# A transformer's last block in steps of two head pairs instead of one, with another order of work on VectorE

## What is computed

```python
h = _rmsnorm(x, norm_g[l]) * (1.0 + scale[:, None, :]) + shift[:, None, :]
p = jnp.einsum('bsd,de->bse', h, w_in[l])
c_val, c_gate, c_og, ts, r_og, g_conv, g_rwkv = jnp.split(p, SPLITS, axis=-1)
# conv branch: 31 taps over time, layer norm, silu, gate, @ w_conv_out
# rwkv branch: r, k, v, decay and rate from ts; per head of 64
def step(state, inp):
    r_t, w_t, k_t, v_t, kk_t, b_t = inp
    sk = jnp.einsum('bhvk,bhk->bhv', state, kk_t)
    state = (state * w_t[:, :, None, :] - sk[..., None] * b_t[:, :, None, :]
             + v_t[..., None] * k_t[:, :, None, :])
    return state, jnp.einsum('bhvk,bhk->bhv', state, r_t)
# group norm per head, bonus, gate, @ w_rwkv_out
m = jax.nn.sigmoid(g_conv) * y_conv + jax.nn.sigmoid(g_rwkv) * y_rwkv
x = x + gate[:, None, :] * jnp.einsum('bsd,de->bse', m, w_out[l])
```

## Time and profile before

| | us |
|---|---|
| median of 3 runs | 1036.68 (1036.30 to 1037.82) |
| the profiled execution, its own time | 1036.78 |
| its span, first to last instruction | 1035.0 |
| PE busy (matmul) | 1002.3 (97%) |
| weight loads | 932.6 (90%) |
| DVE busy | 869.7 (84%) |
| ACT busy | 604.3 (58%) |
| loads from HBM | 164.83 MB |

### The profile page before, as it was taken

One profiled execution on the slowest core, in us unless ns is written; L12 is line 12 of the kernel. 1 busy time (PEld: TensorE's weight loads), 2 busy tenths in 40 slices (PEclk: granted clock), 3 DMA queues, 4 the chain that ended last, 5 costly groups with the idle time before them and its releaser, 6 DMA issues.

```text
span 1035.0 us, 25000 instructions
## 1 busy us (share of the span) xinstructions
PE 1002.3 (97%) x10690; PEld 932.6 (90%) x10690; DVE 869.7 (84%) x1447; ACT 604.3 (58%) x875; POOL 18.4 (2%) x38
## 2 busy tenths in 40 slices
PE   7999999999999999999999999999999999899997
PEld 6999999999999989989898998889999998789996
DVE  7866699899988886999899897989999999965474
ACT  7755664444446756554444577556657676686443
POOL 2000000000000000000000000000000000000000
PEclk9999999999999999999999999999999999999999
DMA  9662457777554515576775646334323422234531
GB/s 283 214 203 94 152 189 252 230 243 227 199 176 149 164 47 181 200 231 227 241 234 182 203 133 194 109 99 124 122 86 123 125 84 84 84 124 155 170 126 41
DMA packets 136075, 168.26 MB, mean 163 GB/s; under 512 B 3216, under 2 KB 125328, under 8 KB 135728
## 3 DMA queue, kind: packets, MB, share of 16 engines
q1 hardware_dynamic: 132080, 153.44, 46.1%
q0 software_dynamic: 3904, 13.50, 4.0%
HBM read 164.83 MB, written 2.10 MB: 161 GB/s over the span
## 4 chain that ended last, share of the span: by engine, by line
PE 68%; DVE 22%; ACT 6%; issue 2%; DMA 2%; SPq 0%; DVEq 0%; ACTq 0%
PE banks L353 13%; PE banks L318 8%; PE banks L319 7%; PE banks L320 7%; PE banks L355 7%; DVE hf L2652 4%; DVE w_parts L304 3%; DVE w_parts L280 3%; PE banks L655 2%; PE bank L657 2%; PE bank L655 2%; PE banks L657 2%; PE bank L659 2%; PE banks L659 2%; ACT w_parts L275 1%
## 5 line engine op out<-in xcount | busy, mean ns | idle before, releaser
L280 DVE TENSOR_TENSOR w_parts<-raw,w_parts 128x2048 fp32r<-128x2048 f32 x95 | 217.1, 2288 | 27.3 <-ACT w_parts L275 26.8
L353 PE MATMUL banks<-x_parts,w_parts 128*128 128x512 f32 x640 | 227.1, 399 | 0.0
L318 PE MATMUL banks<-x_parts,w_parts 128*128 128x256 f32 x704 | 211.9, 301 | 0.0
L319 PE MATMUL banks<-x_parts,w_parts 128*128 128x256 f32 x736 | 208.3, 283 | 0.0
L320 PE MATMUL banks<-x_parts,w_parts 128*128 128x256 f32 x704 | 199.1, 283 | 0.0
L275 ACT ACTIVATE w_parts<-raw 128x2048 fp32r<-128x2048 f32 x95 | 180.9, 1905 | 3.6 <-PE banks L810 2.1
L355 PE MATMUL banks<-x_parts,w_parts 128*128 128x256 f32 x640 | 179.8, 281 | 0.0
L353 PEld LDWEIGHTS banks<-x_parts,w_parts 128*128 128x128 f32 x640 | 120.3, 188 | 29.0
L319 PEld LDWEIGHTS banks<-x_parts,w_parts 128*128 128x128 f32 x736 | 141.2, 192 | 0.5 <-issue 0.5
L318 PEld LDWEIGHTS banks<-x_parts,w_parts 128*128 128x128 f32 x704 | 134.5, 191 | 7.6 <-issue 0.7
L320 PEld LDWEIGHTS banks<-x_parts,w_parts 128*128 128x128 f32 x704 | 134.8, 192 | 0.0
(11 more groups left out here) (418 smaller groups left out, 2411.6 us busy)
## 6 DMA issues: line engine op xcount, KB each, us to landing
raw<-in_ffn_w_up SPq DMA_DIRECT2D x44, 1024.0 KB, 5.1
raw<-in_w_in SPq DMA_DIRECT2D x36, 1024.0 KB, 5.5
raw<-in_ffn_w_down SPq DMA_DIRECT2D x22, 1024.0 KB, 5.9
big<-in_ada_w_t POOLq DMA_DIRECT2D x24, 512.0 KB, 4.1
raw<-in_gla_w_in SPq DMA_DIRECT2D x11, 1024.0 KB, 5.6
raw<-in_attn_w_qkv SPq DMA_DIRECT2D x6, 1024.0 KB, 4.9
raw<-in_gla_w_out SPq DMA_DIRECT2D x4, 1024.0 KB, 5.5
raw<-in_attn_w_out SPq DMA_DIRECT2D x4, 1024.0 KB, 4.9
```

Of the source, the lines that this page charges most:

```text
L280: eng.tensor_tensor(WL[:, n % RING, :, :], RAW[:, n % RING, :, :], WH[:, n % RING, :, :].bitcast(F32), ALU.subtract).then_inc(w_lo_ready, 1)
L318: nc.tensor.matmul(ps, wh, xh, start=start, stop=False)
L319: nc.tensor.matmul(ps, wh, xl, start=False, stop=False)
L353: nc.tensor.matmul(PS[bank + m].rearrange("p (a t) -> p a t", a=2), WH[:, s, k, ms], XP[:, :, k, :], start=k == 0, stop=False, skip_group_ ...
```

## The change

The last block goes in steps s = −2 to 4 of 13 slots, and in each step the chain, the middle and the front serve two pairs (a "duo"). Fronts of the second pair of a duo follow the first in the same step, in slots 6 to 11. Inverse masks, copies and evacuations of both pairs are made by one instruction. The blocks are dealt anew: 4, 5, 6, 6, 5 and 9 in steps −2 to 3. The hi halves stand at unit 7 of the block two earlier and unit 0 of the block before, the lo halves at units 2 and 4 of the block before. The lo of most blocks is written over the raw weights (`RAW_LO`), which frees 24 tiles (`DUO`) for the second pair; the load of block n + 3 then waits for the matmuls of block n. DVE has the front ahead of `slot(s, r)`. Taps start in slot 8 of step −2 and end with step 2. rout 0 and 1 are whole blocks behind the steps.

```diff
 STEP_BLOCKS = {
     -3: _blocks("r0 k0 v0"),
-    -2: _blocks("val0 gate0"),
-    -1: _blocks("r1 k1 v1 val1"),
-    0: _blocks("gate1 val2 rog0 gate2"),
-    1: _blocks("r2 k2 v2 val3"),
-    2: _blocks("gate3 rog1 gr0 gr1"),
-    3: _blocks("r3 k3 v3 gr2"),
-    4: _blocks("rog2 gr3 gc0"),
-    5: _blocks("gc1 gc2"),
-    6: _blocks("rog3 og0 og1 og2 og3"),
-    7: _blocks("gc3 cout0 cout1 cout2 cout3"),
-    8: _blocks("rout0 rout1 rout2 rout3 out0 out1 out2 out3"),
+    -2: _blocks("val0 gate0 k1 r1"),
+    -1: _blocks("v1 val1 gate1 k2 r2"),
+    0: _blocks("v2 val2 gate2 k3 r3 gc0"),
+    1: _blocks("rog0 v3 val3 gate3 gr0 gc1"),
+    2: _blocks("rog1 gr1 gr2 gr3 gc2"),
+    3: _blocks("rog2 gc3 og0 og1 og2 og3 rog3 cout0 cout1"),
+    4: _blocks("cout2 cout3 rout0 rout1 rout2 rout3 out0 out1 out2 out3"),
 }
...
+DUOS, SLOTS = 4, 13
+LO_IN_RAW = range(N_L3 + 3, N_ROUT + 1)
...
+        def w_lo(n):
+            return (RAW_LO if n in LO_IN_RAW else WL)[:, n % RING, :, :]
...
         def load(sp, n, src, i=0):
-            if n >= RING:
+            if n - RING in LO_IN_RAW:
+                sp.wait_ge(block_done, n - RING + 1)
+            elif n >= RING:
                 sp.wait_ge(w_lo_ready, n - RING + 1 + RING * i)
...
-        def put_blocks(s, names, last=24):
+        def put_blocks(s, names, last=2 * SLOTS):
             per = 8 * len(names)
             for b, name in enumerate(names):
                 n = PLACE[name]
                 for u in range(8):
                     q = (8 * b + u) * last // per
                     put_at(s, q, ("unit", n, u))
-                    if u % 2 == 0:
-                        put_at(s, q, ("hi" if u < 4 else "lo", n + 2, u // 2 % 2))
+                    if u == 0 and n > N_L3 + 3:
+                        put_at(s, q, ("hi", n + 1, 1))
+                    if u in (2, 4) and n > N_L3 + 3:
+                        put_at(s, q, ("lo", n + 1, u // 2 - 1))
+                    if u == 7:
+                        put_at(s, q, ("hi", n + 2, 0))
                 put_at(s, q, ("take", n))
-                put_at(s, min(q + 1, 23), ("use", n))
-
-        for s in range(-2, 8):
+                put_at(s, min(q + 1, 2 * SLOTS - 1), ("use", n))
+
+        for s in range(-2, 4):
             put_blocks(s, STEP_BLOCKS[s])
...
+        put_blocks(4, STEP_BLOCKS[4][:2], 10)
+        for j, q in enumerate((11, 14, 16, 19)):
+            put_at(3, q, ("conv_y_hi", j))
+            put_at(3, q + 1, ("conv_y_lo", j))
+        for k, q in enumerate((0, 1, 2, 4, 5, 6, 7)):
+            put_at(3, q, ("ln", k))
+        TAP_FIRST, TAP_SLOTS = 16, 10 + 4 * 2 * SLOTS
         for k in range(TAP_SLOTS):
             q = TAP_FIRST + k
-            put_at(q // 24 - 1, q % 24, ("taps", TAPS * k // TAP_SLOTS, TAPS * (k + 1) // TAP_SLOTS))
-        put(4, 10, ("three_pairs",))
-
+            put_at(q // (2 * SLOTS) - 2, q % (2 * SLOTS), ("taps", TAPS * k // TAP_SLOTS, TAPS * (k + 1) // TAP_SLOTS))
+        put(2, 0, ("three_pairs",))
```

The front's small matmuls on PE are interleaved with the y and x parts:

```diff
                 if c == 0:
                     pe.wait_ge(sem("kk_sums_kept"), p + 1)
                     pe.wait_ge(sem("rkrk_ready"), p + 1)
-                for rows in HEADS:
-                    last = nc.tensor.matmul(PS[2][rows, cols64(c)], blk[rows, rows], TMP[rows, cols64(c)], start=True,
-                                            stop=True)
+                    if p % 2:
+                        pe.wait_ge(sem("sigmoids_ready"), 2 * p + 2)
+                    elif p // 2 == DUOS - 1:
+                        pe.wait_ge(sem("gn_rstd"), 1)
+                last = head_sums(TMP, c, 0)
...
+            def front_pieces(d, r, i):
+
+                if not 0 <= d < DUOS:
+                    return
+                if r == 6:
+                    if i == 0:
+                        pe.wait_ge(sem("bonus_kept"), 2 * d + 1)
+                    decay_piece(2 * d + 1, i, T)
+                elif r == 8:
+                    if i == 0:
+                        pe.wait_ge(sem("kk_sums_kept"), 2 * d + 2)
+                    rate_piece(2 * d + 1, i, 2, T)
+                elif i < NC and r in (3, 7):
+                    kk_sums(2 * d + r // 7, i)
+                elif i < NC and r in (5, 9):
+                    rkrk_sums(2 * d + r // 9, i)
...
+            def later_slots(p, q, s, r):
+                if 0 <= p < DUOS:
+                    chain_hop(p, r)
+                for i, (e, c) in enumerate(PARTS):
+                    if 0 <= p < DUOS:
+                        chain_part(p, r, i)
+                    if 0 <= q < DUOS and r % 2:
+                        y_part(q, (r - 3) // 2, e, c)
+                    elif 0 <= q < DUOS:
+                        x_part(q, (r - 4) // 2, e, c)
+                    front_pieces(s + 2, r, i)
+                    norm_pieces(s - 1, s, r, i)
+                if r == 12 and 0 <= q < DUOS:
+                    turn_v(q)
```

ACT and DVE:

```diff
+            def front(d, r):
+                first, second = 2 * d, 2 * d + 1
                 if r == 0:
...
+                    decay_sigmoid(first, 0)
+                    rate_sigmoid(first, 6, 0)
+                elif r == 4:
+                    kk_root(first)
+                elif r == 5:
+                    decay_exps(first)
                 elif r == 6:
...
+                    keys_scaled(second)
+                    decay_sigmoid(second, T)
+                elif r == 8:
+                    rate_sigmoid(second, 2, T)
+                    kk_root(second)
+                elif r == 10:
+                    decay_exps(second)
...
+                for r in range(SLOTS):
+                    if r == 11 and s + 3 < DUOS:
+                        keys_scaled(2 * (s + 3))
+                        nc.scalar.preload_act_table(ACT.Sigmoid)
+                        loaded[0] = "sigmoid"
+                    if 0 <= s < DUOS:
                         chain(s, r)
-                    if r == 10 and 0 <= s + 1 < 8:
-                        turned_v(s + 1)
-                    if 0 <= s + 1 < 8:
+                    if 0 <= s + 1 < DUOS:
                         middle(s + 1, r)
+                        if r == 12:
+                            turned_v(s + 1)
                     slot(s, r)
-                    if s + 2 < 8 and (s, r) != (-2, 0):
+                    if s + 2 < DUOS and (s, r) != (-2, 0):
                         front(s + 2, r)
-                    if 1 <= s:
-                        gn(s - 1, r + 8 if s == 8 else r)
+                    if 1 <= s < DUOS:
+                        gn(s - 1, s, r)
+                    elif s == DUOS:
+                        gn_last(r)
                     if 2 <= s and r == 0:
```

```diff
+            def front(d, r):
+                first, second = 2 * d, 2 * d + 1
+                if r == 3:
+                    kk_kept(first)
+                    keys_mixed(first)
+                elif r == 4:
+                    cumulated(first)
                 elif r == 5:
...
+                    bonus(first)
+                    keys_normed(first)
+                elif r == 6:
+                    keys_decayed(first)
                 elif r == 7:
...
+                    kk_kept(second)
                 elif r == 8:
...
+                    keys_mixed(second)
                 elif r == 9:
...
+                    cumulated(second)
+                    bonus(second)
+                elif r == 10:
+                    keys_normed(second)
+                elif r == 11:
+                    keys_decayed(second)
...
+            for s in range(-2, 5):
+                for r in range(SLOTS):
+                    if 0 <= s < DUOS:
                         chain(s, r)
-                    if 0 <= s + 1 < 8:
+                    if 0 <= s + 1 < DUOS:
                         middle(s + 1, r)
                     if (s, r) == (-2, 3):
                         front(0, 3)
                         use_block(N_L3 + 2)
+                    if s + 2 < DUOS and (s, r) != (-2, 3):
+                        front(s + 2, r)
                     slot(s, r)
...
+                    if 1 <= s < DUOS and r == 5:
+                        gn(2 * s - 2, GNS[0])
+                    elif 1 <= s < DUOS and r == gn_second(s) + 1:
+                        gn(2 * s - 1, GNS[0])
+                    elif s == DUOS and r == 2:
+                        gn(2 * DUOS - 2, GNS[0])
+                        gn(2 * DUOS - 1, GNS[1])
...
+            split_lo_whole(N_ROUT + 1)
+            split_lo_whole(N_ROUT + 2)
             dve.wait_ge(sem("cout_used"), 4)
             mix(0)
-            mix(1)
             split_lo_whole(N_ROUT + 3)
             m_lo(0)
+            mix(1)
+            split_lo_whole(N_OUT)
             m_lo(1)
-            split_lo_whole(N_OUT)
             mix(2)
             split_lo_whole(N_OUT + 1)
+            m_lo(2)
             mix(3)
-            m_lo(2)
             m_lo(3)
             split_lo_whole(N_OUT + 2)
             split_lo_whole(N_OUT + 3)
```

894 lines of the change are left out of this document (455 added, 439 removed).

## The result

The change makes the kernel slower: 1061.53 us in the median (1060.42 to 1062.32, 4 runs) against 1036.49 (1036.11 to 1037.82), a ratio of 1.0238 with an interval of 1.0221 to 1.0256. The profiled execution took 1062.21 us with a span of 1060.4. Forecast were 1030.8 us and a gain.

A forecast was written before the change was run, and what follows sets the result against it. PE bounds four-block steps, DVE those with fewer. 622.6 + 91.8 + 64.3 + 64.0 + 51.5 + 126.4 + 8.5 = 1029.1 us span, with 1.8 around it 1030.8 (−16 mode changes, +10 new waits); range 1021 to 1042.

The forecast's parts named there:

- Fewer mode changes: Last block: full-array runs followed by small ones 72 times instead of 112, at 0.40 us each: −16 us of PE time.
- The new wait: Second front, slots 6 to 9: PE waits 3.3 and 2.6 us, DVE 4.3 in step 0; 13 us taken in all.
- The clock: Rival: two waits in each of four steps, each followed by half clock, add 13.6 us: 1044.4 us; chance 0.05.
- The list of hops: Second front, slots 6 to 9: ACT's queue delays the sigmoids; PE waits 3.3 and 2.6 us in step 0.
- VectorE in steps −2 and −1: DVE full from about 21 us into step −2, with 1.3 us of waits; both steps take 91.8 us.
- Small matmuls: PE's small matmuls per double step: 18 us, but 14.5 in step −1 and 16 in step 2; one pair 9.0.
- The part from step 3 on: PE's 19 blocks 109.4, 15 mode changes 6.0, small matmuls about 6 and waits 5: 126.4 us.
- the price that I named for losing the cover of the loads: Loads wait for the block three before to be multiplied; covered, otherwise about 1 us for each of the last ten blocks.
- Lockstep: Rival: each slot in steps −1 to 2 lasts as long as its longer engine, 13 us over forecast: 1043.8; chance 0.13.
- A table load: ACT's queue in slot 6: 1.28 us without a drain; by the skill's 2.66 the time would be 3 us later.

The follow-up runs named there:

- e7: Changed kernel with one unit of a weight block put amid the small matmuls in slots 3 to 12 of steps −1 to 2, restoring mode changes: 1080.86 us.
- e1: Changed kernel with the second pair's scaled keys and sigmoids ahead of ScalarE's weight work in slots 6 and 8: 1047.40 us.
- e6: Changed kernel with each convolution tap from the second on computed for 64 of 256 columns only: 1047.46 us.
- e4: Changed kernel with 24 and 16 useless full-array matmuls at the start of slots 7 and 9 in steps 0 and 1: 1056.32 us.
- e10: e9 with taps dealt 14, 46, 56, 60, 72 over steps −2 to 2, spread evenly over half slots, and `three_pairs` moved: 1044.01 us.
- e11: e10 with the split of the convolution's output ahead of the weight halves in slots 9 and 10 of step 3, on ScalarE and VectorE: 1037.79 us.
- e12: e11 with a block's rounded halves on ScalarE half a slot to a slot earlier, the remainders left where they were: 1036.57 us.
- e9: e1 with slot 4's front, and step 1's group-norm root in slot 4, also ahead of that slot's weight work on ScalarE: 1047.01 us.

## Why the prediction was wrong

**Fewer mode changes: right.** −16 by the rows, −13 to −16 by step 2 of e7.

**The new wait: right, in slots 7 to 9.** Forecast 3.3 and 2.6 us on PE and 4.3 on DVE in step 0; the trace has 3.46, 2.27 and 4.73. In step 1 they were 5.4 in the forecast and are 3.46 and 1.54. e1 and e6 show that the queue's order causes it and VectorE's load has no part in it.

Five steps of it failed: the half clock was left out of the sum, one hop was missing from the list, VectorE's idle time in steps −2 and −1 and the small matmuls were put too small, and one late part of the convolution was not seen.

**The clock: left out of the sum.** I priced the half clock behind each wait, 1.7 us, and gave it a chance of 0.05, as if it were an accident of one place. In the trace of after it follows all eight waits of 2.0 us and more, and e4 shows that the waits cause it. The Trainium skill's rule (TensorE: Matmul & The Clock Gate, HAM oscillation — how this bites in real kernels), that an engine which waits on every pass is throttled on every pass, agrees with this trace, PEclk 0.95 in four steps. It isn't a certainty for each wait: 3.45 us in e6 and 2.64 in e10 and e11 passed without. Its whole price: 5% of 33.4, 64.7, 69.2 and 74.3 us, and 3% of 132.5, make 16 us, an upper bound since PE stood still for part of it; before, it was 1.6. In steps 0 and 1 it is 5 to 6 us, by the 1.4 of e4 for each of four falls.

**The list of hops: one was missing.** I looked for readers of the second pair's sigmoids only. In step 1 slot 5 PE also waits 4.18 us for the group norm's root, which stands in ACT's queue behind two halves, an evacuation and a table load, exactly as the sigmoids do. It costs 4.2 us, and 5 to 6 with its half clock, of the 10.3 by which step 1 was missed.

**VectorE in steps −2 and −1: nearly full, but not without waits.** I let it be full from 21 us into step −2 (643.6) on, with 1.3 us of waits. VectorE alone from there to the start of step 0 (window, length, busy, granted clock):

```profile
643.60:656.05 12.45, 9.61 (x22) 0.89 0.29 88
656.05:720.75 64.70, 61.00 (x124) 0.95 0.28 83
```

It is busy 70.6 us, against 69.5 in the forecast (19.1 + 55.2, less the 4.8 by which it ends after PE's start of step 0), and idle 6.5. So the sum was nearly right, although step −1 alone looks larger than its 55.2: its window holds 12 halves of remainders and 62 taps where the table gives it 10 and 57, since VectorE runs late. The idle time was missed: 3.5 us for a sigmoid (L1990) and 2.4 for an evacuation (L1911), both ScalarE's. e6 (56.0) and e10 (59.9) show that less work on VectorE shortens step −1. The waits of PE there (3.2 for a remainder, 3.0 for a mask) and two drops of the clock are what it looks like from PE's side.

**Small matmuls: 18 a step was too little, and this is the largest term.** I doubled one pair's 9.0. Step 2, with a full clock and 1.07 us of waits, shows it best: they take 20.3 us (the sum over their load starts, the wait left out) where I had 16. By the same sum step 0 has 21.8 (in e1, at full clock) for my 18, and step 1 22.8 to 24.0. About half of this is the 9.0 itself: in step 2 of the kernel before the sum gives 10.0 for one pair, and what I took there for 1.4 us of waits were small matmuls. The other half is that each costs more in the change, 0.022 us (20.3 for 912) instead of 0.019 (10.0 for 515). The weight loads of a y part of the change, alone in its slot:

```profile
895.25 0.14 PEld L1351 LDWEIGHTS bank<-pair_tiles,duo_tiles 64*64 64x64 f32 x2
895.29 1.02 PEld L1268 LDWEIGHTS bank<-big,duo_tiles 64*64 64x64 f32 x32
896.38 0.19 PEld L328 LDWEIGHTS banks<-x_parts,w_parts 128*128 128x128 f32 x1
```

and an x part of before, whose two lines use the straight and the crossed quarters of the array in turn:

```profile
744.75 0.14 PEld L1220 LDWEIGHTS banks<-big 64*64 64x64 f32 x2
744.76 0.14 PEld L1223 LDWEIGHTS banks<-big 64*64 64x64 f32 x2
...
745.15 0.14 PEld L1220 LDWEIGHTS banks<-big 64*64 64x64 f32 x2
745.16 0.14 PEld L1223 LDWEIGHTS banks<-big 64*64 64x64 f32 x2
745.37 0.19 PEld L318 LDWEIGHTS banks<-x_parts,w_parts 128*128 128x128 f32 x1
```

To the next full load, mode change included, 32 loads take 1.09 us on one diagonal alone (895.29 to 896.38) and 0.62 where both alternate (744.75 to 745.37). Two loads on one diagonal cost 0.059 us, four on both 0.055. Before, a pair's y part had the chain's or the front's matmuls between most of its own (the order of before, above, shows it with the kk sums); in the change the y part is twice as long and its company is not. The diagonal is read from the traces; no run changed it alone.

**The part from step 3 on: one late part of the convolution.** It took 132.5 us to the last full matmul for 126.4 forecast, and PE waits 4.04 us in it (974.59 to 978.63), with 6.8 us of half clock. Loads are not the cause. ScalarE's part (L1958) is ready at 974.47, but VectorE's (L2799) stands in the queue behind two remainders, and the second of these waits for a half that ScalarE starts only at 974.53, behind its other work:

```profile
973.85 0.62 ACT L1958 ACTIVATE conv_y_parts<-hf 128x512 fp32r<-128x512 f32 x1
974.53 1.06 ACT L306 ACTIVATE w_parts<-raw 128x1024 fp32r<-128x1024 f32 x1
975.62 2.36 DVE L314 TENSOR_TENSOR raw_lo<-raw,w_parts 128x1024 fp32r<-128x1024 f32 x2 [3.63 <-ACT w_parts L306]
977.89 0.69 DVE L2799 TENSOR_TENSOR conv_y_parts<-hf,conv_y_parts 128x512 fp32r<-128x512 f32 x1
```

e11 changes this order alone, against e10, and the part falls from 132.2 to 126.6, as forecast. In e11 ScalarE waits 18 us for the loads of cout and rout, as in the change (18.6), and PE waits for remainders there for 2.2 us in either. So of the price that I named for losing the cover of the loads, 1 us for each of the last ten blocks, at most these 2.2 us show; no run puts the old way of loading back. What the late loads do is to limit a repair, as e12 shows.

**Lockstep** had 0.13, 1043.8 us and the right sign. Its picture, each slot as long as its slower engine, is not what happened: in e6 VectorE's sums shrink by 18% and steps 0 and 1 by 2% and 1%. e9 does show its cause, a remainder one slot before its block, as what blocks a repair in step 0.

The terms that failed add up, as an estimate from these sums: VectorE's waits in steps −2 and −1 6; small matmuls 4 in each of steps 0, 1 and 2, in step 1 rather 5; the clock in steps 0 and 1 5 to 6; the missing hop 4; the part from step 3 on 6. That is 33 to 35, less some 2 by which other waits were shorter than forecast, against 31 missed. The new waits themselves, which the prediction named as what works against the gain, came as forecast.

## What to carry to other kernels

Fusing two passes to save a fixed cost per pass also halves the time in which short results must travel between engines: list every reader in the fused pass, on each its place in the producer's queue, and add to each wait what the clock can take behind it. Add up what the small pieces cost from their own starts, not from what a step leaves over. Put short work that another engine waits for ahead of long work that nobody waits for yet, but only with slack behind the long work: here four instructions moved in each step gave 14 us, and moving the rest gave 10 of them back. The order alone, on the old structure, gave 2.9 us, more than the restructuring with five repairs (1036.57).

## What the runs showed of the hardware

- 80 useless full-array matmuls, placed in waits, made a kernel 5.2 us faster in the median, and 4.1 us faster in the two steps that got them: behind the filled waits the clock stayed at 2.4 GHz (e4).
- The clock doesn't fall behind every such wait: 3.46 us in slot 7 of step 0 with a fall in the change, 3.45 in the same place without one in e6; 2.64 without in e11, 2.48 with in e12.
- A change between full-array and 64x64 matmuls and back costs 0.40 us by the loads, and 0.32 of a step's time where ten were added to a step without other waits (e7, step 2). The Trainium skill (TensorEngine Tiling (Array Packing), Key Properties) says that a change of mode drains the array, without a figure; the trace agrees, 0.33 us from a full load to a small one and 0.21 back, where full loads are 0.12 apart.
- 64x64 weight loads seem to cost by diagonal: 0.059 us for two on one, 0.055 for two on each, in both kernels' traces.
- A table load was 1.28 us again in front of gate2 (754.62), with no drain to be seen beside it: the next instruction starts 1.29 us after the load's start. The 2.66 us of the Trainium skill (ScalarE: Activation LUTs, What ACT_TABLE_LOAD costs) are not borne out, and the wait was as forecast without the drain.
